# Five reorderings in a decoder layer on one core, and who splits the weights beside the stick-breaking steps

## Time and profile before

| | us |
|---|---|
| median of 2 runs | 2007.13 (2006.51 to 2007.76) |
| the profiled execution, its own time | 2005.29 |
| its span, first to last instruction | 2003.2 |
| PE busy in the span | 1947.3 (97%) |
| DVE, POOL, ACT busy | 1067.7, 945.7, 737.5 |
| mean granted PE clock | 0.993 of full |

### The profile page before, as it was taken

The page is one execution under the profiler, slowest core; times in us unless marked ns, Lnnn a source line. Parts: engine busy times, 40 slices in busy tenths (PEclk is TensorE's granted clock), DMA queues, the critical chain, the costliest instruction groups (busy, mean ns, idle before and its releaser), DMA issues. The chain is left out here.

```text
span 2003.2 us, 25014 instructions
## 1 busy us (share of the span) xinstructions
PE 1947.3 (97%) x9622; PEld 1618.1 (81%) x9622; DVE 1067.7 (53%) x1167; ACT 737.5 (37%) x1165; POOL 945.7 (47%) x519
## 2 busy tenths in 40 slices
PE   7999999999999999999999999999999999999996
PEld 6888888788877787888889988877888888888886
DVE  5577585700057777338862227776455454412856
ACT  2323223300035555412463343554333433423443
POOL 4243342343445554534575533576455554544551
PEclk9999999999999999999999999999999999999998
DMA  5121120122200000311322212332222222364462
GB/s 193 32 84 52 63 84 31 43 74 72 83 23 23 31 22 32 115 54 63 116 85 73 73 53 63 109 113 100 90 74 85 90 74 89 127 211 142 141 199 74
DMA packets 56535, 168.17 MB, mean 84 GB/s; under 512 B 5888, under 2 KB 12160, under 8 KB 55424
## 3 DMA queue, kind: packets, MB, share of 16 engines
q1 hardware_dynamic: 49648, 142.86, 21.6%
q10 hardware_dynamic: 6800, 24.12, 3.2%
HBM read 142.84 MB, written 24.12 MB: 83 GB/s over the span
## 5 line engine op out<-in xcount | busy, mean ns | idle before, releaser
L509 POOL TENSOR_TENSOR w_hi<-w_raw,one 128x1024 fp32r<-128x1024 f32 x68 | 134.5, 1978 | 459.0 <-PE unit L661 459.0
L661 PE MATMUL unit<-x_hi,w_hi 128*128 128x512 f32 x768 | 247.9, 394 | 11.7 <-DVE diag L1845 9.5
L671 PE MATMUL unit<-x_lo,w_hi 128*128 128x512 f32 x768 | 245.5, 390 | 0.4 <-POOL x_lo L528 0.4
L679 PE MATMUL unit<-x_hi,w_lo 128*128 128x512 f32 x768 | 190.3, 390 | 0.0
L661 PEld LDWEIGHTS unit<-x_hi,w_hi 128*128 128x128 f32 x768 | 144.0, 189 | 44.1 <-issue 12.2
L512 POOL TENSOR_TENSOR w_lo<-w_raw,w_hi 128x1024 fp32r<-128x1024 f32 x68 | 176.3, 2592 | 5.4
L671 PEld LDWEIGHTS unit<-x_lo,w_hi 128*128 128x128 f32 x768 | 144.1, 188 | 31.1 <-POOL x_lo L528 0.8
L679 PEld LDWEIGHTS unit<-x_hi,w_lo 128*128 128x128 f32 x768 | 144.6, 188 | 30.1
L573 POOL TENSOR_TENSOR w_lo<-w_raw,w_hi 128x1024 fp32r<-128x1024 f32 x46 | 112.3, 2442 | 85.4 <-ACT w_hi L1445 85.0
L591 POOL TENSOR_TENSOR beta<-beta,stick 128x128 f32<-128x128 f32 (+7 forms) x64 | 78.4, 1227 | 126.8 <-DVE stick L1984 126.8
L1984 DVE TENSOR_TENSOR_SCAN stick<-stick 128x128 f32<-128x128 f32 (+7 forms) x64 | 106.5, 1665 | 48.1 <-ACT stick L1369 47.9
(11 more groups left out here) (604 smaller groups left out, 4945.7 us busy)
## 6 DMA issues: line engine op xcount, KB each, us to landing
w_raw<-stream SPq DMA_DIRECT2D x157, 512.0 KB, 3.6
w_next<-stream SPq DMA_DIRECT2D x34, 512.0 KB, 4.3
hidden_store<-hidden SPq DMA_DIRECT2D x22, 512.0 KB, 2.6
h_raw<-hidden_store SPq DMA_DIRECT2D x44, 256.0 KB, 3.4
rope_sb<-rope ACTq DMA_DIRECT2D x8, 1024.0 KB, 5.0
w_next<-stream SPq DMA_DIRECT2D x12, 384.0 KB, 3.4
acc<-xT ACTq DMA_DIRECT2D x8, 512.0 KB, 9.9
ret_branch<-acc ACTq DMA_DIRECT2D x8, 512.0 KB, 2.6
```

What stands on the lines that cost most here:

```text
L509: pool.tensor_tensor(w_hi[s][:, 0:width], w_raw[:, s, 0:width], one[:].to_broadcast([P, width]), ALU.mult).then_inc(w_hi_done, 1)
L661: x = pe.matmul(out, w_hi[s][:, wk], hi[:, k, cols], start=k == 0, stop=False, skip_group_check=True)
L671: last = pe.matmul(out, w_hi[s][:, wk], lo[:, k, cols], start=False, stop=k == kts - 1 and x_lag > w_lag, skip_group_check=True)
L679: last = pe.matmul(out, w_lo[s][:, wk], hi[:, k, cols], start=False, stop=k == kts - 1 and x_lag <= w_lag, skip_group_check=True)
```

## The change

Six edits, with no matmul added or taken away.

1. **Low inputs**: the projections of the retention output get `lags=(4, 0)`: the input's low parts follow 4 k later, the weight's low parts at once.
2. **Value products**: `sb_values` is cut in `high_values` and `low_values`; `high_values(g-1, 0)` goes before `turn_w(g-1, 1)`.
3. **Fill**: for the first pair two k before the first logits, two more at qt = 0, one in each slot at qt = 1 and 2. For the other pairs two k at qt = 0, one in each slot at qt = 1, two in each at qt = 2. The first k of the next pair's chunk thus comes a step earlier, at qt = 0.
4. **Splits beside the steps**: ACT makes the high part at the end of step qt = 2, 4, 6, before it copies the values out; POOL makes the low part in the next step, between its two `beta` products.
5. **Early output tiles**: in the last memory head `begin_tile(0)` goes before the first turn of probabilities and `begin_tile(1)` between the two (15 matmuls each: high by high and weight's low part for k = 0..5, input's low part for k = 0..2); `low_tiles` does the other three k later. The value products of this head go to other banks, DVE makes the low parts of a later, and ACT stores the head's result in other pieces (`store_last`, `last_stored`).
6. **Weight forms**: forms 8 and 9 are split ahead of the last third of the input sums on ACT and POOL, the sums for S2 and S1 ahead of two `turn_lo` and a hidden product on DVE; on ACT forms 10 and 11 go ahead of the four `turn_hi_parts(n, (3,))`.

```diff
@@ pool, the steps
-                    if g in FILL_SPLITS:
-                        (single_lo if hd else single_hi)(FILL_SPLITS[g])
+                    if hd == 0 and g - 1 in FILL_SPLITS:
+                        single_lo(FILL_SPLITS[g - 1])
@@ pool, entry of the FFN
-            for n in range(QUART):
+            for n in range(QUART - 1):
                 turn_lo(n)
-            for f in range(2 * RING, FORMS):
+            form_lo(2 * RING)
+            form_lo(2 * RING + 1)
+            turn_lo(QUART - 1)
+            for f in range(2 * RING + 2, FORMS):
                 form_lo(f)
@@ pe, retention output
-                project(..., ret_hi, ret_lo, arrived=(ret_hi_done, ret_split))
+                project(..., ret_hi, ret_lo, arrived=(ret_hi_done, ret_split), lags=(4, 0))
@@ pe, the steps
+                if g == 0:
+                    fill(0, range(2))
                 if g < STEPS:
                     logits(g)
                     fill(*fill_slot(g, 0))
...
                 if g:
+                    high_values(g - 1, 0)
                     turn_w(g - 1, 1)
-                    sb_values(g - 1, 0)
+                    low_values(g - 1, 0)
                     if g < STEPS:
                         fill(*fill_slot(g, 1))
-                    sb_values(g - 1, 1)
+                    high_values(g - 1, 1)
+                    low_values(g - 1, 1)
@@ pe, last memory head
+            def begin_tile(q):
+                pe.wait_ge(unit_drained[q], U_MO // 2 - 1)
+                pe.wait_ge(w_hi_done, CH_MO + q + 1)
+                pe.wait_ge(n2.a_hi, KT - 2)
...
+                pe.wait_ge(n2.a_split, 3)
...
+                else:
+                    begin_tile(0)
                 turn_p(0)
...
+                else:
+                    begin_tile(1)
                 turn_p(1)
@@ act, the steps
                     if g in FILL_ENDS:
                         drain_fill(FILL_ENDS[g])
+                    if g in FILL_SPLITS:
+                        single_hi(FILL_SPLITS[g])
@@ act, entry of the FFN
             turn_hi_parts(2, range(3))
-            turn_hi_parts(3, range(3))
-            plain_gate(0, 1)
             form_hi_part(8)
             form_hi_part(9)
+            plain_gate(0, 1)
+            turn_hi_parts(3, range(3))
             plain_gate(1, 0)
+            form_hi_part(10)
+            form_hi_part(11)
             act.wait_ge(unit_ready, U_FFN + PLAIN_PRODUCTS - 2)
             for n in range(QUART):
                 turn_hi_parts(n, (3,))
-            form_hi_part(10)
-            form_hi_part(11)
             plain_gate(1, 1)
@@ dve, last memory head
-                    for k in range(3):
-                        split_a(n2, 0, k)
                 least(0)
+                if not more:
+                    split_a(n2, 0, 0)
                 least(1)
                 invert_sums(0)
+                if not more:
+                    split_a(n2, 0, 1)
+                    split_a(n2, 0, 2)
                 invert_sums(1)
@@ dve, entry of the FFN
             turn(3)
+            weight_sum(PLAIN, 0)
+            weight_sum(PLAIN, 1)
             turn_lo(2, 2)
             turn_lo(3, 2)
             plain_hidden(0, 1)
-            weight_sum(PLAIN, 0)
-            weight_sum(PLAIN, 1)
@@ fill_slot
-    per = 0 if qt == 0 else 2 if qt < 3 else 4
-    first = 4 * (qt == 2) + per * slot
-    return 6 * p + FILL_USE[qt], range(first, first + per)
+    if qt > 2:
+        ks = range(4 * slot, 4 * slot + 4)
+    elif qt == 0:
+        ks = range(0 if slot else 2 * (p == 0), 0 if slot else 2 + 2 * (p == 0))
+    elif qt == 1:
+        first = 2 + 2 * (p == 0) + slot
+        ks = range(first, first + 1)
+    else:
+        per = 1 if p == 0 else 2
+        ks = range(8 - 2 * per + per * slot, 8 - per + per * slot)
+    return 6 * p + FILL_USE[qt], ks
```

More of the change, by code:

```diff
@@ L563, in single @@
                                    ).then_inc(w_split, 1)
[L565 to L569, removed]
             def single_lo(c):
@@ L787, in _ @@
                 u = free_unit(U_GRET + 2, 2, n, 0)
-                project(n * 2 + (CH_GRET + 2), 0, halves(u), ret_hi, ret_lo, arrived=(ret_hi_done, ret_split)).then_inc(unit_ready, 1)
+                project(n * 2 + (CH_GRET + 2), 0, halves(u), ret_hi, ret_lo, arrived=(ret_hi_done, ret_split), lags=(4, 0)
+                        ).then_inc(unit_ready, 1)
                 u = free_unit(U_GRET + 2, 2, n, 1)
@@ L847, in values_split, with both_parts, high_values, low_values @@
                     pe.wait_ge(unit_drained[1], U_SB // 2 + 2)
-            def sb_values(g, hd):
+            def both_parts(p, hd, b):
+                return sv[p % 2][:, 2 * b + hd, :, :].rearrange("p a d -> p (a d)")
+            def high_values(g, hd):
                 p, qt = divmod(g, QT)
+                if qt % 2 == 0:
+                    return
                 pe.wait_ge(wt_hi, 2 * g + hd + 1)
+                for b in range(qt + 1):
+                    q0 = P if b == qt else 0
+                    pe.matmul(aux[:, 2, hd * 2 * P + q0:(hd + 1) * 2 * P], both_parts(p, hd, b),
+                              wT_hi[:, hd, b, q0:2 * P], start=False, stop=False, skip_group_check=True)
+            def low_values(g, hd):
+                p, qt = divmod(g, QT)
                 if hd == 0:
@@ L857, in sb_values @@
                 c0 = hd * 2 * P + qt % 2 * P
[L859 to L866, removed]
                 pe.wait_ge(wt_split, 2 * g + hd + 1)
@@ L942, in sums, with low_tiles @@
                 x.then_inc(m.sums_taken, 1)
+            def begin_tile(q):
+                pe.wait_ge(unit_drained[q], U_MO // 2 - 1)
+                pe.wait_ge(w_hi_done, CH_MO + q + 1)
+                pe.wait_ge(n2.a_hi, KT - 2)
+                for k in range(KT - 2):
+                    pe.matmul(residual_bank(q), w_hi[q][:, k * P:(k + 1) * P], a_hi[0][:, k, :], start=k == 0, stop=False,
+                              skip_group_check=True)
+                pe.wait_ge(w_split, CH_MO + q + 1)
+                for k in range(KT - 2):
+                    pe.matmul(residual_bank(q), w_lo[q][:, k * P:(k + 1) * P], a_hi[0][:, k, :], start=False, stop=False,
+                              skip_group_check=True)
+                pe.wait_ge(n2.a_split, 3)
+                for k in range(3):
+                    pe.matmul(residual_bank(q), w_hi[q][:, k * P:(k + 1) * P], a_lo[0][:, k, :], start=False, stop=False,
+                              skip_group_check=True)
+            def low_tiles(q):
+                pe.wait_ge(n2.a_split, KT - 2)
+                for k in range(3, KT - 2):
+                    pe.matmul(residual_bank(q), w_hi[q][:, k * P:(k + 1) * P], a_lo[0][:, k, :], start=False, stop=False,
+                              skip_group_check=True)
             def residual(m, chunk, first):
@@ L950, in residual @@
                 for q in range(2):
-                    pe.wait_ge(unit_drained[q], first // 2)
-                    tiles(q, range(KT - 2), begins=q == 0)
+                    if m is n2:
+                        low_tiles(q)
+                    else:
+                        pe.wait_ge(unit_drained[q], first // 2)
+                        tiles(q, range(KT - 2), begins=q == 0)
                 for q in range(2):
@@ L1014, in values @@
                     u = free_unit(base, XU, h, k)
+                    if more:
+                        outs = [u[:, dt * HALF:(dt + 1) * HALF] for dt in range(2)]
+                    elif hf == 0:
+                        free_unit(base, XU, h, 1)
+                        outs = [unit[:, dt, half(1)] for dt in range(2)]
+                    else:
+                        outs = [aux[:, dt, :] for dt in range(2)]
                     pe.wait_ge(turn_hi, h * 3 + (hf + 2))
                     for dt in range(2):
-                        out = u[:, dt * HALF:(dt + 1) * HALF]
+                        out = outs[dt]
                         for mt in range(2):
@@ L1035, in mem_head @@
                 pe.wait_ge(turn_split, h * 3 + 1)
-                scores(0, ends_chunk=more)
+                scores(0, ends_chunk=True)
                 scores(1)
@@ L1044, in mem_head @@
                     mem_chunk(h + 1, 3, u, 1).then_inc(unit_ready, 1)
+                else:
+                    begin_tile(1)
                 turn_p(1)
                 values(0, 2 if more else 0)
-                values(1, 3 if more else 1)
+                values(1, 3 if more else 0)
                 if more:
@@ L1392, in drain_fill, with single_hi @@
                                    ).then_inc(fill_hi, 1)
+            def single_hi(c):
+                act.wait_ge(w_loaded[c % 2], (c // 2 + 1) * 16)
+                act.wait_ge(chunk_started, c)
+                act.activation(w_hi[c % 2][:], w_raw[:, c % 2, :], ACT.Copy).then_inc(w_hi_done, 1)
             act.wait_ge(acc_saved, 16 * KT)
@@ L1440, in split_a @@
```

(13 more changed lines are left out.)

20 lines of the change are left out of this document (13 added, 7 removed).

## The result

The changed kernel takes **2031.12 us** (median of 2 runs, 2028.96 to 2033.27) against 2007.13: ratio 1.0123, 95% interval 1.0101 to 1.0146. A second measurement gave 2030.11 against 2007.33, ratio 1.0117 (1.0100 to 1.0134). I had said 2022, in a range of 1993 to 2029: the sign was right, the time lies 2 us above the range. The profiled execution took 2033.27 us, its span 2031.5: 28.0 us more than the profiled execution of before, 4 to 5 more than the medians differ.

A forecast was written before the change was run, and what follows sets the result against it. The prediction took PE, busy 97% of the span, as the bound, with some 56 us idle to win. Its terms, -1.7 + 23.5 - 8.6 + 3.0 = +16.2 us, gave 2021.5 or 2023.3, stated as 2022, range 1993 to 2029.

The forecast's parts named there:

- start of the steps: First stick-breaking steps: two k before the logits and two more hide PE's waits for vT and beta; -1.6 us.
- qt = 3 to 4: Entry to step qt = 4: the fill waits for POOL's low part, +1.6 us, 4 times, 6.4.
- qt = 5 to 6: Entry to step qt = 6: the fill waits for POOL's low part, +2.0 us, 4 times, 8.0.
- pair boundaries: Between head pairs: late low part delays the second head's turn; +3.2 us, 3 times, 9.6, at full clock.
- end: End of the steps: beta 0.3 later and ACT's split no longer covered by high_values, +0.8; +1.1 us.
- last memory head: From the last scores to the third output tile: early tiles fill PE's waits and keep the clock; -8.6 us.
- weight forms: Ahead of product S2: 2.9 us before A11 go, but PE stands 6.4 us until ACT's hold; +3.0 us.
- Up to 3 x 2.2 more: 2029: Rival at the pair boundaries: the clock falls there too, up to 3 x 2.2 us more, 2029 us; chance 0.10.
- its two k fewer win nothing: Step after the boundary's first: its 5.76 us chain is not PE's, so less fill there gains nothing.
- POOL's order: In the steps: a waiting DVE scan goes before POOL's next instruction, so the low part ends about 2.3 us after it.
- POOL goes first: Rival in the steps: the low part starts at once behind beta, before the scan; in all +4.3, 2011 us; chance 0.13.
- The low parts come in time: Rival in the steps: the low part ends before PE's fill asks; in all -14.4, 1993 us; chance 0.22.

The follow-up runs named there:

- steps alone: The kernel before with only the edits to the stick-breaking steps (fill, high values moved ahead, splits on ACT and POOL): 2039.93 us, ratio 1.0165.
- old dealing of the fill: The changed kernel with the later pairs' fill dealt as before in their first three steps (none, two, two tiles a slot): 2018.23 us, ratio 1.0062.
- memory alone: The kernel before with only the edits to the last memory head and the residual's first tiles: 1998.56 us, ratio 0.9964.
- forms alone: The kernel before with only the order of the weight forms changed: 2009.0 us, ratio 1.0013.
- the stall filled: The changed kernel with 12 unused matmuls in the stall at each of the three later pairs' first fill: 2023.42 us, again 2024.41 us.
- the five kernels with the low part or both splits moved: The changed kernel with POOL's low part ahead of both beta products (1999.74 us), and four combined versions with the old forms order (ratios 0.9956 to 0.9969).
- the low part first: The changed kernel with only POOL's low part moved ahead of the step's two beta products: 1999.74 us, ratio 0.9968.
- the four last kernels: Gaining edits with old forms order: low part ahead of the products (1997.30 us) or both splits on POOL as before (1998.93); each with early A11 copy (2000.82, 1999.79).

## Why the prediction missed

By its own terms, from the shifts between the two traces (first profile):

| term | predicted | measured |
|---|---|---|
| low inputs | -1.7 | -2.3 |
| start of the steps | -1.6 | -1.7 |
| qt = 3 to 4 | +6.4 | +5.0 (0.5, then 1.5 three times) |
| qt = 5 to 6 | +8.0 | +8.0 |
| **pair boundaries** | **+9.6** | **+21.9** |
| end | +1.1 | +1.3 |
| last memory head | -8.6 | -8.5 |
| weight forms | +3.0 | +2.6 |

The measured column adds up to +26.3, where the two spans differ by 28.3. Of the rest 1.2 us come at 1057.63, where PE waits 0.89 us for a weight whose DMA landed later; the second profile has no such wait. The equal numbers at qt = 5 to 6 are made otherwise than I said: 1.6 us four times at the fill of qt = 6, and 0.35 four times in step qt = 5.

**The step that failed** is "I take +3.2 us, 3 times, 9.6", and in it the clock. The sum priced the boundary at full speed and left the fall to a rival: "Up to 3 x 2.2 more: 2029", chance 0.10. The stall itself was right: 2.81 us, and with its clock restored the boundary's first step is 2.9 us longer than before. The runs put 2.9 to 4.3 us on top of it, three times, 9 to 12 in all: with these the 2022 would have been 2031 to 2034. Two readings led there.

First, I sorted waits by length, "A wait of 3.2 us went with a clock of 0.81, pieces up to 2.9 us with 1.00", and took 3.1 for undecided. The windows behind that were of one execution. Over all profiled executions length alone does not sort them:

| wait of PE in front | in | the clock fell at |
|---|---|---|
| 2.8 us, boundary | changed kernel twice, steps alone | 9 of 9 |
| 2.9 us, boundary | old dealing of the fill | 2 of 3 |
| 2.06 us, boundary | before, memory alone, forms alone (steps as before) | 4 of 9 (0, 2, 2) |
| 1.5 to 1.6 us, qt = 4 and 6 | the six profiles with the low part between the products | 4 of 42 |

Two of these. In the kernel with the memory edits alone, the wait of the earlier trace rows at the first boundary, and its window; the step took 8.70 in place of 7.43 us:

```profile
628.96 1.72 PE L830 MATMUL aux<-ident,beta 128*128 128x128 f32 x8 [2.06 <-POOL beta L592]
```

```profile
625.00:638.00 13.00, 10.94 (x81) 0.87 0.01 1
```

In the changed kernel, second profile, qt = 4 of the third pair; the step took 12.35 in place of 10.78 us:

```profile
733.55 0.47 PE L887 MATMUL aux<-x_lo,w_hi 128*128 128x512 f32 x1 [1.50 <-POOL w_lo L568]
...
734.55 0.63 PE L887 MATMUL aux<-x_lo,w_hi 128*128 128x512 f32 x1
```

So the profile of before was lucky at its boundaries, and the 12.4 us are counted from that.

Second, I said of the thinner fill of qt = 1 and 2 that "its two k fewer win nothing", but not what they lose: where before had one wait of 0.66 us, the changed kernel has four of 0.2 to 0.8 us ahead of step qt = 2, and by the end of the last of them, or up to 1.4 us behind it, the second dip begins. Thin fill and stall together gave it at 9 boundaries of 9 (the same three profiles). With the stall filled it came at one of three, in both profiles; with thin fill and no stall at 4 of 15 (the five kernels with the low part or both splits moved); with the old dealing at none of three, though a wait of 2.9 us was left.

By parts, first profile: stall 3 x 2.9 = 8.7, clock 12.4, and 0.8 for the three steps qt = 7 just ahead of the boundaries (I had charged 0.3 for each to ACT), together the 21.9.

**POOL's order** carried the forecast, and held. The low part always ended about as worked out behind the scan that it met: 629.29 against the scan's 627.15, 2.14 us, where I had said 2.3. Timeline of DVE in the changed kernel, against the earlier trace rows:

```profile
601.43 2.61 DVE L2038 TENSOR_TENSOR_SCAN stick<-stick 128x768 f32<-128x768 f32 x1
...
623.82 3.33 DVE L2038 TENSOR_TENSOR_SCAN stick<-stick 128x1024 f32<-128x1024 f32 x1
```

The low part issued at 602.38 ended at 606.19, 2.15 us behind the first of these. "POOL goes first" would have had the scan come behind it; it did at none of the 11 places. That the two do not run together this trace shows both ways: beside the first of these scans the low part took 3.81 us, against 2.40 alone, and beside the `beta` at 629.25 (2.00 us) the scan of 128 columns that started 0.07 us behind it took 2.20 us, against 0.41 alone. "The low parts come in time" fell by the waits at all 11 places, save that pair 0 had only 0.5 us at qt = 4. ACT's high part was held up nowhere: 1.05 to 1.10 us at all 12 places, 1.10 beside a scan and a `beta` (575.42).

**The memory head** went as said: window 18.66 us at 1.00 where the last lines of the prediction had 18.5. **The forms** too, and for the reasons given:

```profile
1387.96 0.77 PE L1150 MATMUL unit<-t_hi,w_hi 128*128 128x512 f32 x1 [6.07 <-ACT held L1748]
```

A stop of 6.07 us (6.4 predicted), and behind it the matmuls of S2 take 5.17 us (1387.96 to 1393.13) where they took 2.83 (1361.85 to 1364.68): 2.3 us of clock, where I had charged 2.2; the window over that stretch showed 0.58. For the shorter waits no length of idle time divides the cases: 2.90 us left the clock full once, and in the case below it fell to 0.68 with no wait longer than 0.75 us.

## What to carry to other kernels

When a stall is new on the engine that sets the time, price it twice: its length, and the slower matmuls behind it (here 2.9 us, and 2.9 to 4.3 us more). That price is an average over executions: behind 2.06 us of waiting the window of before showed 1.00, that of the kernel with the memory edits alone 0.87. And don't take filling work out of the steps that follow: with less of it behind the stall the second dip came at 9 boundaries of 9, with the old dealing at none of three. Place a helper's work by what stands idle on its engine: the same subtraction cost some 30 us (2030 to 2031 against 1999.74) between two products that wait for another engine, and nothing ahead of them. And when only the consumer is moved, ask what else is queued behind the late instruction: here the wait went from the fill to `beta`.

## What the hardware showed beyond that

- **A fall without a long wait.** With the low part first no wait at the boundaries is longer than 0.76 us, and still the clock dips. Timeline and windows of PE in that kernel:

```profile
633.40 0.30 PE L828 MATMUL aux<-ident,beta 128*128 128x128 f32 x1 [0.17 <-DVE wT_lo L2044]
...
635.24 0.27 PE L872 MATMUL aux<-wT_lo,sv 128*64 128x128 f32 x1 [0.68 <-DVE wT_lo L2044]
...
636.27 0.44 PE L828 MATMUL aux<-ident,beta 128*128 128x128 f32 x2 [0.75 <-POOL beta L588]
```

```profile
634.00:636.60 2.60, 1.17 (x6) 1.00 0.00 0
636.60:642.00 5.40, 5.40 (x24) 0.68 0.00 0
642.00:650.00 8.00, 8.00 (x46) 1.00 0.22 66
```

  PE had been busy for 1.17 of 2.60 us before it fell. It cost 1.5 us at two of the three boundaries, none at the other, where the same waits stand. Two of the four last kernels had such a dip at one boundary, the other two at none.
- **The same stall, another dip.** In the changed kernel 2.81 us of waiting gave 0.76 then 0.72 in one execution and 0.88, 0.74, 0.98 in the other: the clock's part of a loss has its own spread, here 12.4 against 9.2 us.
- **What two engines cost each other.** POOL's low part of 128x1024 takes 2.40 us alone and, in the changed kernel, 3.30, 3.81 and 4.33 beside scans of 512, 768 and 1024 columns; the scan of 1024 columns ends after 3.33 us beside a `beta` product, where 2.29 was seen alone.
